# Spacers between the SBUF buffers of a two-layer encoder step: operands and one weight slot start 32 bytes into a 64-byte block

## The chip, the cores and the metric

The kernel runs on one NeuronCore of a Trainium2 chip, as one launch. The metric is the device time of the whole launch in microseconds. SBUF is the on-chip memory of 128 partitions; a buffer has the same start address in each partition, and all addresses below are bytes within a partition.

## The reference

One inference step of a two-layer encoder trunk for two request groups that share the weights: 256 prompt tokens and 32 sample tokens, model width 1024. Every layer adds four parts to the residual x:

```
x = x + 0.5 * swiglu(rmsnorm(x, norm_g[0]), w1g, w1u, w1d)      # width 2816
x = x + mix(rmsnorm(x, norm_g[1]))                              # layer 0: attention, layer 1: recurrent
x = x + 0.5 * swiglu(rmsnorm(x, norm_g[2]), w2g, w2u, w2d)
x = x + (p_i @ w_pe) * sigmoid(rmsnorm(x, norm_g[3]) @ w_pg)
```

The mixer of layer 0 is stick-breaking attention (16 heads of 64, with 256 past keys for the sample group). The mixer of layer 1 is a width-4 convolution, two block-diagonal gates (16 blocks of 80), a linear recurrence over time and a gelu gate, 1280 wide. A final rmsnorm follows. All inputs and outputs are float32.

## The kernel before, in words

**Layout.** Activations lie transposed: features on the 128 partitions, the 288 tokens (TOK) along the free axis, so a buffer such as `xg_hi` is 128 x 8 x 288. A weight matrix is cut into tiles of 128 x 128 that are the stationary operand of a matmul; a row block of 288 tokens is the moving operand. Both are 4 bytes per element.

**Three matmuls per tile.** Each float32 operand is split into a high part and a low part of the type float32r. `product` (L1086) multiplies one tile as hi x hi (L1090), moving low x weight high (L1091), moving high x weight low (L1092), all into one PSUM bank. Each of the three loads its stationary tile anew. What follows calls these three a tile.

**Phases.** `plan` (L72) lists the phases in order: up0, down0 (the first half-step), qkv, wo (attention), up1, down1, ple0, up2, down2, lru_in, gates, lru_g, lru_o, up3, down3, ple1. A phase is a row of groups; a group is one load of weights (16 tiles in up, qkv, lru_in; 11 in down; 10 in ple and lru_o; 13 in gates). Groups alternate between two slots, `raw0`, `w_hi0`, `w_lo0` and `raw1`, `w_hi1`, `w_lo1`. For a group ahead, SP loads the weights into `raw` (L303 on), ACT copies them rounded into `w_hi` (L476), and DVE subtracts to get `w_lo` (L736), each in two parts; TensorE waits for `w_lo_done`. ACT starts on a slot when TensorE is done with the group before in that slot (`tiles_done`), and SP loads when DVE is done with `raw`.

**Moving operands by phase.** Stages 0 to 3 and 5 to 7 read `xg_hi`, `xg_lo` (the residual times the norm's gain). Stage 4, that is up2, reads the second pair `xg_side_hi`, `xg_side_lo`. The down phases read `h_hi`, `h_lo`, wo reads `o_hi`, `o_lo`, gates reads `c_hi`, `c_lo` (292 columns instead of 288), lru_o reads `y_hi`, `y_lo`. A ple group has first two tiles on `p_hi`, `p_lo` and then eight on `xg_hi`, `xg_lo`.

**Where the buffers start.** `sb` (L147) takes buffers one behind the other; each begins at the next multiple of 32 bytes. The first, `x_res`, begins at 16512, a multiple of 64. A row of 288 tokens is 1152 bytes, 18 x 64, so each of a buffer's rows has the start of the buffer within a block of 64. Before the change `xg`, `raw`, `w_hi`, `w_lo`, `h`, `xg_side`, `o` and `y` all begin at a multiple of 64. `vecs_sb` holds 648 bytes, which puts `p_hi` and `p_lo` and all the small buffers behind them up to `mean_w` (`square`, `sum_squares`, `std`, `rstd`, `gate_in`, `gate_act`, `up_in`, `hidden0`, `hidden1`) in the middle, 32 bytes past a multiple of 64. A row of `c_hi` or `c_lo` is 1168 bytes, so its rows begin 0, 16, 32 and 48 bytes past one in turn. A weight tile is 512 bytes.

The scoped buffers (L185 to L223) share addresses: `h`, `xg_side`, `p_raw` and `first_squares` in one scope, the attention's in the next, the recurrent block's in a third.

Of the kernel before, what the change touches and what calls it, by code (L numbers as in the profile page):

```python
# [6 lines left out]
F32 = mybir.dt.float32  # L7
F32R = mybir.dt.float32r
# [3 lines left out]
P = 128  # L12
# [14 lines left out]
TOK = SEQ + DEC  # L27
KD = D_MODEL // P
# [115 lines left out]
def build(nc, a):  # L144
    ctx = ExitStack()
    with ctx:
        def sb(name, shape, dt=F32, scope=ctx):  # L147
            return scope.enter_context(nc.sbuf_tensor(name, shape, dt))
# [5 lines left out]


        x = sb("x_res", [P, KD, TOK])
        xg_main = (sb("xg_hi", [P, KD, TOK], F32R), sb("xg_lo", [P, KD, TOK], F32R))
        raw = [sb(f"raw{i}", [P, 2 * KD * P]) for i in range(2)]
        w_hi = [sb(f"w_hi{i}", [P, 2 * KD * P], F32R) for i in range(2)]
        w_lo = [sb(f"w_lo{i}", [P, 2 * KD * P], F32R) for i in range(2)]  # L160
        vecs = sb("vecs_sb", [P, sum(VECS.values())])
        vec, at = {}, 0
        for n, w in VECS.items():
# [19 lines left out]


        with ExitStack() as scope:  # L185
            h_hi = sb("h_hi", [P, KF, TOK], F32R, scope)
            h_lo = sb("h_lo", [P, KF, TOK], F32R, scope)
            xg_side = (sb("xg_side_hi", [P, KD, TOK], F32R, scope), sb("xg_side_lo", [P, KD, TOK], F32R, scope))
            p_raw = sb("p_raw", [P, 2 * KP, TOK], F32, scope)
            first_squares = sb("first_squares", [P, KD // 2, TOK], F32, scope)  # L190
        with ExitStack() as scope:
            o_hi = sb("o_hi", [P, KD, TOK], F32R, scope)
            o_lo = sb("o_lo", [P, KD, TOK], F32R, scope)
            q_all = sb("q_all", [P, PAIRS, TOK], F32, scope)
            k_all = sb("k_all", [P, PAIRS, KEYS], F32, scope)
            v_all = sb("v_all", [P, PAIRS, 3 * P], F32, scope)
            past_v = sb("past_v_sb", [P, PAST // P, D_MODEL], F32, scope)
            v_rows = [sb(f"v_rows{i}", [P, 3 * P], F32, scope) for i in range(2)]
            logit = [[sb(f"logit{i}{j}", [P, SCOLS], F32, scope) for j in range(2)] for i in range(2)]
            stay = [[sb(f"stay{i}{j}", [P, SCOLS], F32, scope) for j in range(2)] for i in range(2)]  # L200
            stay_hi = [[sb(f"stay_hi{i}{j}", [P, SCOLS], F32R, scope) for j in range(2)] for i in range(2)]
            stay_lo = [[sb(f"stay_lo{i}{j}", [P, SCOLS], F32R, scope) for j in range(2)] for i in range(2)]
            mask = sb("mask", [P, SCOLS], F32, scope)
            all_ones = sb("all_ones", [P, P], F32, scope)
            from_here = sb("from_here", [P, P], F32R, scope)
            ones = sb("ones", [P, P], F32R, scope)
            ident = sb("ident", [P, P], F32, scope)
# [1272 lines left out]
```

## Time and profile before

| | |
|---|---|
| median of 3 runs | 1229.05 us (1228.37 to 1229.31) |
| profiled execution | 1229.69 us |
| its span, first to last instruction | 1227.8 us |
| granted TensorE clock over the span | 0.990 of full |
| TensorE busy | 1188.5 us (97%) |
| VectorE (DVE) busy | 790.1 us (64%) |
| ScalarE (ACT) busy | 582.5 us (47%) |
| DMA | 193.20 MB, mean 157 GB/s |

The profiled execution lies 0.6 us above the median of the runs, and 1.9 us of it lie around the span. A matmul's bar in the profile overlaps the next one's, so the rate of TensorE is not read from the length of a bar but from the distance between the starts of two matmuls; this text calls that distance the pitch.

### The profile page before, as it was taken

Reading aid. Unit: us, or ns where it says so; the run is one execution under the profiler, and the core shown is the slowest. Engines: PE = TensorE matmul, PEld = TensorE weight load, DVE = VectorE, ACT = ScalarE, POOL = GpSimd, SP = SyncE. Lnnn points to the kernel's source line nnn. Section 1 sums busy time; section 2 is a strip of 40 time slices with the busy share of each in tenths; the row PEclk is TensorE's granted clock in tenths of the full one; section 3 lists DMA queues with packets and bytes.
Section 4 is the critical chain, followed back from the end, with each engine's and each line's share of the span. In section 5 each row is a group of like instructions: output and inputs, shape, how many; then the busy total and the mean of one; then the engine's idle time right before and its main releaser. Section 6 shows DMA issues by size and latency. Waiting matters only on the chain.

```text
span 1227.8 us, 23251 instructions
## 1 busy us (share of the span) xinstructions
PE 1188.5 (97%) x8952; PEld 1177.0 (96%) x8952; DVE 790.1 (64%) x1161; ACT 582.5 (47%) x860; POOL 177.4 (14%) x204
## 2 busy tenths in 40 slices
PE   6999999889999999999999999999996999999996
PEld 6999999889999999999999999999996999999996
DVE  7656555566649666655786666456889765665566
ACT  6444443445555444433564444344674544443353
POOL 3000011211124000002230000021245400000122
PEclk9999999899999999999999999999998999999998
DMA  6554444633343544444455444445452544444542
GB/s 221 181 171 156 145 152 165 240 104 104 104 146 138 176 166 171 150 145 162 153 191 183 155 165 149 160 148 195 147 172 88 188 171 165 152 152 143 181 145 96
DMA packets 35899, 193.20 MB, mean 157 GB/s; under 512 B 3808, under 2 KB 6128, under 8 KB 22784
## 3 DMA queue, kind: packets, MB, share of 16 engines
q1 hardware_dynamic: 34800, 187.86, 44.6%
q0 software_dynamic: 1040, 4.51, 1.1%
q8 instruction: 42, 0.69, 0.2%
q14 instruction: 17, 0.14, 0.0%
HBM read 188.78 MB, written 3.58 MB: 157 GB/s over the span
## 4 chain that ended last, share of the span: by engine, by line
PE 85%; DVE 7%; issue 2%; ACT 2%; POOL 2%; DMA 2%; SPq 0%; DVEq 0%; POOLq 0%; ACTq 0%
PE bank L1090 28%; PE bank L1092 27%; PE bank L1091 27%; DVE w_lo L736 2%; DMA raw<-in_up 1%; ACT w_hi L476 1%; PE bank L1135 1%; POOL sum_squares L341 1%; DVE xg_lo L745 1%; PE bank L1121 1%; DVE u_ext L868 1%; POOL gated L427 1%; DMA raw<-in_lru_o 0%; DVE y_lo L859 0%; DVE u_ext L870 0%
## 5 line engine op out<-in xcount | busy, mean ns | idle before, releaser
L476 ACT ACTIVATE w_hi<-raw 128x1024 fp32r<-128x1024 f32 (+2 forms) x410 | 370.4, 927 | 364.4 <-PE bank L1092 345.2
L736 DVE TENSOR_TENSOR w_lo<-raw,w_hi 128x1024 fp32r<-128x1024 f32 (+2 forms) x410 | 452.8, 1122 | 91.5 <-ACT w_hi L476 88.5
L1090 PE MATMUL bank<-xg_hi,w_hi 128*128 128x288 f32 x1536 | 460.1, 300 | 14.4 <-DVE w_lo L767 8.7
L1091 PE MATMUL bank<-xg_lo,w_hi 128*128 128x288 f32 x1536 | 455.6, 297 | 0.0
L1092 PE MATMUL bank<-xg_hi,w_lo 128*128 128x288 f32 x1536 | 454.1, 296 | 0.0
L1090 PEld LDWEIGHTS bank<-xg_hi,w_hi 128*128 128x128 f32 x1536 | 290.2, 189 | 17.1 <-issue 8.7
L1092 PEld LDWEIGHTS bank<-xg_hi,w_lo 128*128 128x128 f32 x1536 | 291.7, 190 | 0.0
L1091 PEld LDWEIGHTS bank<-xg_lo,w_hi 128*128 128x128 f32 x1536 | 290.9, 189 | 0.3
L1090 PE MATMUL bank<-h_hi,w_hi 128*128 128x288 f32 x704 | 208.4, 296 | 0.0
L1091 PE MATMUL bank<-h_lo,w_hi 128*128 128x288 f32 x704 | 207.7, 295 | 0.0
L1092 PE MATMUL bank<-h_hi,w_lo 128*128 128x288 f32 x704 | 207.0, 294 | 0.0
L909 DVE TENSOR_TENSOR gate_in<-bank,rstd 128x288 f32<-128x288 f32 x88 | 40.3, 458 | 177.9 <-PE bank L1092 177.6
L1092 PEld LDWEIGHTS bank<-h_hi,w_lo 128*128 128x128 f32 x704 | 132.6, 188 | 0.0
L1091 PEld LDWEIGHTS bank<-h_lo,w_hi 128*128 128x128 f32 x704 | 132.2, 188 | 0.0
L1090 PEld LDWEIGHTS bank<-h_hi,w_hi 128*128 128x128 f32 x704 | 131.9, 187 | 0.0
L1090 PE MATMUL bank<-xg_side_hi,w_hi 128*128 128x288 f32 x352 | 104.5, 297 | 0.0
L1091 PE MATMUL bank<-xg_side_lo,w_hi 128*128 128x288 f32 x352 | 103.8, 295 | 0.0
L1092 PE MATMUL bank<-xg_side_hi,w_lo 128*128 128x288 f32 x352 | 103.5, 294 | 0.0
L351 POOL TENSOR_TENSOR sum_squares<-x_res 128x288 f32<-128x288 f32 x8 | 6.2, 779 | 614.3 <-DVE x_res L759 614.3
L481 ACT ACTIVATE xg_hi<-x_res,vecs_sb 128x288 fp32r<-128x288 f32 (+1 forms) x56 | 28.9, 532 | 125.8 <-DVE x_res L759 123.2
L344 POOL TENSOR_TENSOR square<-x_res 128x288 f32 (+1 forms) x58 | 44.5, 767 | 242.5 <-DVE x_res L759 241.0
L1092 PEld LDWEIGHTS bank<-xg_side_hi,w_lo 128*128 128x128 f32 x352 | 66.3, 188 | 0.0
(186 smaller groups left out, 1275.9 us busy)
## 6 DMA issues: line engine op xcount, KB each, us to landing
raw<-in_up SPq DMA_DIRECT2D x87, 1024.0 KB, 4.8
raw<-in_down SPq DMA_DIRECT2D x64, 704.0 KB, 4.0
raw<-in_qkv SPq DMA_DIRECT2D x24, 512.0 KB, 4.4
raw<-in_ple SPq DMA_DIRECT2D x16, 640.0 KB, 3.8
raw<-in_lru_in SPq DMA_DIRECT2D x6, 1024.0 KB, 4.9
raw<-in_lru_o SPq DMA_DIRECT2D x8, 640.0 KB, 3.8
raw<-in_wo SPq DMA_DIRECT2D x4, 1024.0 KB, 4.9
raw<-in_lru_g SPq DMA_DIRECT2D x4, 1024.0 KB, 4.9
```

The lines of the kernel that those rows point to most:

```text
L341: nc.gpsimd.tensor_tensor(sum_squares[:], sum_squares[:], term, ALU.add).then_inc(summed_squares, 1)
L344: nc.gpsimd.tensor_tensor(square[:], x[:, k, :], x[:, k, :], ALU.mult).then_inc(squared, 1)
L427: nc.gpsimd.tensor_tensor((a_square, gated)[half][:, m, :], rate[:, half * HALF + m, :], rate[:, half * HALF + m, :], ALU.mult).then_inc(a ...
L476: nc.scalar.activation(w_hi[slot][:, cols], raw[slot][:, cols], ACT.Copy).then_inc(w_hi_done, 1)
L481: nc.scalar.activation(xg_of(stage)[0][:, k, :], x[:, k, :], ACT.Copy, scale=gain[:, stage, one(k)]) \
L736: nc.vector.tensor_tensor(w_lo[slot][:, cols], raw[slot][:, cols], w_hi[slot][:, cols].bitcast(F32), ALU.subtract).then_inc(w_lo_done, 1)
L745: nc.vector.scalar_tensor_tensor(out=dst, in0=src, scalar=scalar, in1=hi.bitcast(F32), op0=ALU.mult, op1=ALU.subtract).then_inc(done, 1)
L868: nc.vector.tensor_tensor_scan(u_ext[:, m, 0:SEQ], rate[:, m, 0:SEQ], conv[:, m, 0:SEQ], 0.0, ALU.mult, ALU.add)
L909: nc.vector.tensor_tensor(gate_in[:], first, rstd[:], ALU.mult).then_inc(gate_in_done, 1)
L1090: nc.tensor.matmul(out, w_hi[slot][:, cols], hi[:, k, 0:width], start=start, stop=False)
L1091: nc.tensor.matmul(out, w_hi[slot][:, cols], lo[:, k, 0:width], start=False, stop=False)
L1092: return nc.tensor.matmul(out, w_lo[slot][:, cols], hi[:, k, 0:width], start=False, stop=stop)
```

## The change

Spacer buffers that nothing reads or writes are allocated between the others, and the two weight slots are taken in the order hi0, lo0, hi1, lo1 instead of hi0, hi1, lo0, lo1. No instruction, wait, loop or transfer is added or taken away. The recurrent block's scope has no spacer.

```diff
         x = sb("x_res", [P, KD, TOK])
+        sb("gap0", [P, 8])
         xg_main = (sb("xg_hi", [P, KD, TOK], F32R), sb("xg_lo", [P, KD, TOK], F32R))
+        sb("gap1", [P, 8])
         raw = [sb(f"raw{i}", [P, 2 * KD * P]) for i in range(2)]
-        w_hi = [sb(f"w_hi{i}", [P, 2 * KD * P], F32R) for i in range(2)]
-        w_lo = [sb(f"w_lo{i}", [P, 2 * KD * P], F32R) for i in range(2)]
+        w_hi, w_lo = [sb("w_hi0", [P, 2 * KD * P], F32R)], [sb("w_lo0", [P, 2 * KD * P], F32R)]
+        sb("gap2", [P, 8])
+        w_hi.append(sb("w_hi1", [P, 2 * KD * P], F32R))
+        w_lo.append(sb("w_lo1", [P, 2 * KD * P], F32R))
+        sb("gap3", [P, 8])
         vecs = sb("vecs_sb", [P, sum(VECS.values())])
...
         with ExitStack() as scope:
+            sb("gap_h", [P, 4], F32, scope)
             h_hi = sb("h_hi", [P, KF, TOK], F32R, scope)
             h_lo = sb("h_lo", [P, KF, TOK], F32R, scope)
-            xg_side = (sb("xg_side_hi", [P, KD, TOK], F32R, scope), sb("xg_side_lo", [P, KD, TOK], F32R, scope))
+            sb("gap_side", [P, 12], F32, scope)
+            xg_side = [sb("xg_side_hi", [P, KD, TOK], F32R, scope)]
+            sb("gap_side_lo", [P, 8], F32, scope)
+            xg_side.append(sb("xg_side_lo", [P, KD, TOK], F32R, scope))
...
         with ExitStack() as scope:
+            sb("gap_o", [P, 8], F32, scope)
             o_hi = sb("o_hi", [P, KD, TOK], F32R, scope)
+            sb("gap_o_lo", [P, 8], F32, scope)
             o_lo = sb("o_lo", [P, KD, TOK], F32R, scope)
```

With the rule of 32 bytes the starts within a block of 64 bytes become:

| buffer | before | after |
|---|---|---|
| x_res, raw0, raw1 | 0 | 0 |
| xg_hi, xg_lo | 0, 0 | 32, 32 |
| w_hi0, w_lo0 | 0, 0 | 0, 0 |
| w_hi1, w_lo1 | 0, 0 | 32, 32 |
| p_hi, p_lo and the small buffers | 32 | 32 |
| h_hi, h_lo | 0, 0 | 32, 32 |
| xg_side_hi, xg_side_lo | 0, 0 | 32, 0 |
| o_hi, o_lo | 0, 0 | 32, 0 |
| y_hi, y_lo | 0, 0 | 0, 0 |
| c_hi, c_lo (first row) | 0, 32 | 0, 32 |
| q_all, k_all, v_all, logit and the rest of the attention | 0 | 0 |

## Rows read from the trace of the kernel before

**Rows 1.** The page: busy time by engine, slices of the span, shares of the chain.

```profile
PE 1188.5 (97%) x8952; PEld 1177.0 (96%) x8952; DVE 790.1 (64%) x1161; ACT 582.5 (47%) x860; POOL 177.4 (14%) x204
...
PEclk9999999899999999999999999999998999999998
...
PE 85%; DVE 7%; issue 2%; ACT 2%; POOL 2%; DMA 2%; SPq 0%; DVEq 0%; POOLq 0%; ACTq 0%
```

**Rows 2.** Groups on TensorE: line, out<-in, shapes, count | busy us, mean ns | idle before.

```profile
L1090 PE MATMUL bank<-xg_hi,w_hi 128*128 128x288 f32 x1536 | 460.1, 300 | 14.4 <-DVE w_lo L767 8.7 <-DVE q_all L779 3.1 <-DVE xg_lo L745 1.9
...
L1090 PE MATMUL bank<-h_hi,w_hi 128*128 128x288 f32 x704 | 208.4, 296 | 0.0
...
L1090 PE MATMUL bank<-xg_side_hi,w_hi 128*128 128x288 f32 x352 | 104.5, 297 | 0.0
...
L1090 PE MATMUL bank<-y_hi,w_hi 128*128 128x288 f32 x80 | 25.2, 315 | 9.3 <-DVE y_lo L859 6.2 <-DVE w_lo L736 3.1
...
L1090 PE MATMUL bank<-o_hi,w_hi 128*128 128x288 f32 x64 | 19.4, 303 | 0.4 <-DVE x_res L759 0.4
```

**Rows 3.** Waits: engine, line, whom it waited for: us in total, times, longest.

```profile
ACT w_hi L476 <- PE bank L1092: 345.2, 134, 8.6
...
DVE gate_in L909 <- PE bank L1092: 177.6, 79, 3.0
...
ACT w_hi L476 <- DMA raw<-in_up: 7.1, 5, 2.9
```

**Rows 4.** Timeline of TensorE in up0: start us, bar us, engine, line, operation.

```profile
40.06 0.29 PE L1090 MATMUL bank<-xg_hi,w_hi 128*128 128x288 f32 x1
...
52.86 0.29 PE L1090 MATMUL bank<-xg_hi,w_hi 128*128 128x288 f32 x1
```

**Rows 5.** Timeline of TensorE in the ple0 phase, start to start.

```profile
605.03 0.29 PE L1090 MATMUL bank<-p_hi,w_hi 128*128 128x288 f32 x1
...
618.58 0.29 PE L1090 MATMUL bank<-xg_hi,w_hi 128*128 128x288 f32 x1
618.70 0.29 PE L1091 MATMUL bank<-xg_lo,w_hi 128*128 128x288 f32 x1
...
624.96 0.29 PE L1090 MATMUL bank<-p_hi,w_hi 128*128 128x288 f32 x1
```

**Rows 6.** Timeline of TensorE in the gates phase: its first and second matmul, and the first behind it.

```profile
879.58 0.30 PE L1090 MATMUL bank<-c_hi,w_hi 128*128 128x292 f32 x1
879.72 0.30 PE L1091 MATMUL bank<-c_lo,w_hi 128*128 128x292 f32 x1
...
900.43 0.29 PE L1090 MATMUL bank<-xg_hi,w_hi 128*128 128x288 f32 x1
```

**Rows 7.** Timeline of TensorE as its clock rises after the up0 phase.

```profile
239.77 0.44 PE L1090 MATMUL bank<-xg_hi,w_hi 128*128 128x288 f32 x1
240.01 0.44 PE L1091 MATMUL bank<-xg_lo,w_hi 128*128 128x288 f32 x1
```

**Rows 8.** Groups on DVE that write a row of 288 columns.

```profile
L910 DVE TENSOR_TENSOR up_in<-bank,rstd 128x288 f32<-128x288 f32 x88 | 39.4, 448 | 0.0
...
L995 DVE TENSOR_TENSOR gate_g<-bank,rstd 128x288 f32<-128x288 f32 x10 | 4.1, 442 | 1.3 <-PE bank L1092 1.3
```

**Rows 9.** Busy us by engine (and count) in two stretches, clock, DMA share, GB/s.

```profile
240.00:400.00 160.00, 154.27 (x1283) 148.00 (x1283) 104.22 (x165) 87.12 (x137) 34.98 (x33) 0.99 0.35 119
...
860.00:970.00 110.00, 100.70 (x734) 99.34 (x733) 93.90 (x145) 68.11 (x103) 47.48 (x49) 0.97 0.41 141
```

**Rows 10.** DMA issues: transfer, count, KB each, median us from issue to landing.

```profile
raw<-in_up SPq DMA_DIRECT2D x87, 1024.0 KB, 4.8
```

## The prediction

> **What bounds the kernel now.** I read the page first: TensorE is busy 97% of the span and carries 85% of the chain that ended last; DVE carries 7%, ACT, POOL and DMA 2% each [rows 1]. The waits agree: ACT waits 345.2 us in total for TensorE to give a weight slot back, and DVE 177.6 us for the sums of an up group, while ACT waits for a load in the up phases for only 7.1 us [rows 3]. A 1 MB load of an up group lands in 4.8 us [rows 10], and the group's 48 matmuls take 6.4 us (below), so transfers are early. TensorE's own rate sets the time, and the rest stands behind it.
>
> So the next view is that rate. The groups of TensorE give the counts: 1536 tiles on xg, 704 on h, 352 on xg_side, 80 on y, 64 on o, three matmuls each [rows 2]; gates has 52 and ple 32 by the code. The bars (about 300 ns) overlap and say nothing of the rate. The timeline does: from 40.06 to 52.86 us lie 96 matmuls, 12.80 us, a pitch of 133.3 ns [rows 4]. At the full clock of 2.4 GHz 288 columns are 120.0 ns, so each matmul takes 13.3 ns, or 32 cycles, more than its columns. This is no fixed cost of an instruction: while the clock was granted at its lower level (1.2 GHz), the pitch is 0.24 us, just its 288 columns [rows 7]. The pitch is also strikingly even: of the triples of matmuls that follow each other without a wait, more than nine in ten take 400 ns to the nanosecond. Something besides the columns holds TensorE back at full clock, and reading operands from SBUF is a candidate. That is what an address can change.
>
> **What the change does, part by part.** No instruction goes or comes. The counts, waits and bytes stay.
>
> *Moving operands.* The trace of before has one operand that already starts mid-block: p. Five ple groups, from 605.03 to 624.96 us, are 150 matmuls in 19.93 us [rows 5]. At the pitch of [rows 4] they would take 20.00 us. They hold 10 tiles on p and 40 on xg, with the same code, slots and clock; the missing 0.067 us are 6.7 ns per p tile, or 2.2 ns per matmul (131.1 ns instead of 133.3). Some of it falls in the xg tiles just behind, where the pitch swings (0.12 us once in [rows 5]) before it is even again, as it also does behind a stall. So p is a disturbance of six matmuls, and what a long stretch of displaced rows settles to is not shown. The second sample is the gates phase, whose rows start at 0, 16, 32 and 48: 156 matmuls of 292 columns in 20.85 us, 133.7 ns [rows 6]. Four more columns are 1.7 ns, so against 133.3 + 1.7 = 135.0 it gains 1.3 ns per matmul; if the columns are not what counts, it loses 0.3 ns.
>
> The bounds for a displaced matmul: below, 120 ns, its columns; above, 140 ns, which the first two of gates show (0.14 us, [rows 6]) and which is also what a count of 16-column blocks gives. (320 cycles are 20 such blocks, 18 of them the row; a displaced row touches 19, so 21 blocks, 336 cycles, 140 ns. The p rows speak against it.) I take the p rows' 2.2 ns, the nearest: same length, same displacement, same instruction.
>
> What it applies to: xg and h, 2240 tiles, all three matmuls displaced: 2240 x 6.7 ns = 15.0 us. xg_side and o, 416 tiles, where the high part is displaced and the low part not, so two matmuls of three: 416 x 2/3 x 6.7 = 1.9 us. y, c and p stay where they are: 0. Together 16.9 us.
>
> *The weight slot.* Slot 1 holds half of the groups, and there weight and moving operand both start mid-block (but for xg_side_lo and o_lo). No row of before shows this: all weight slots start at 0. Two readings are open: what counts is the moving operand's own start (then both slots gain), or that the two reads start apart (then slot 0 alone gains, since in slot 1 both are shifted alike and stand to each other as before). I take the first, by a little, since p's tiles gain in slot 0 and slot 1 alike, and keep the second as a rival.
>
> *What absorbs it.* In the attention (240 to 400 us) TensorE is busy 154.3 of 160 us, in the recurrent block 100.7 of 110 [rows 9]; the chain there runs through DVE and ACT at times. The first holds 192 tiles of qkv and 64 of wo: 256 x 6.7 ns = 1.7 us, of which I strike half, 0.9 us. Elsewhere TensorE has no one to wait for: with a pitch of 131.1 an up group takes 6.29 us, and the 1 MB load lands in 4.8 us.
>
> *DVE, ACT, POOL, SP.* The writes to xg, h, o, w_hi1 and w_lo1 move to mid-block. DVE writes a row mid-block in 448 ns (up_in) and at a block's start in 442 ns (gate_g), both from a bank and rstd [rows 8]: 6 ns, and 1% even of DVE's 7% of the chain is 0.9 us at most; DVE idles 177.6 us for TensorE in the up phases [rows 3], which hides it. I cost it at 0, with 0.9 us kept as the end if that cover goes. The raw buffers move by 64 bytes and stay at a block's start: 0 for the loads, which have 1.6 us of slack per up group. Slots interleaved as hi0, lo0, hi1, lo1 change no instruction: 0.
>
> **The sum.** -16.9 + 0.9 = -16.0 us on the profiled 1229.69 us, that is 1213.7; the median of the runs lies 0.6 us lower, so 1213.
>
> A rule of the Trainium skill speaks against any effect. "SBUF — State Buffer", Specifications, says that SBUF is read in lines of 16 bytes and that crossing into new lines is what costs; 32 bytes are two whole lines, so a displaced row crosses as many as before. By that the sum is 0 and the time 1229; the p rows, 6.7 ns per tile, disagree. "TensorE: Matmul & The Clock Gate", Step-by-step, also has the moving operand and the weight load on two independent read ports, with nothing to collide. Its Back-to-back issue gap puts 288 columns at 122.5 ns; this trace has 133.3, so something that the rule lacks is at work.
>
> **The rivals.**
> *Slot 0 alone gains* (the two reads must start apart): half of the sum, -8 us, 1221. For: it explains why the even 400 ns comes with equal starts, and why the gates, where the starts differ by turns, are in between. Against: nothing in the rows of before.
> *Nothing* (the p rows' gain is a passing disturbance, and long stretches settle at 400 ns again): 1229. For: xg's pitch behind a stall swings as well and then settles. This is what both rules above would give. A change that doesn't do what it says is part of this: if the starts that matter were in units other than 64 bytes, p would not have differed.
> *A new, lower level.* Behind a stall or behind p single pitches are 0.12 us [rows 5], so TensorE can start matmuls closer. If displaced rows settle near 126 ns, 7 ns go from each of 2240 x 3 + 416 x 2 = 7552 matmuls: -53 us, 1176.
> *Slower: slot 1 pays.* In slot 1 weight tile and row both straddle blocks: 9 blocks instead of 8 and 19 instead of 18. If those matmuls, half of 7552, take the 140 ns of [rows 6], that is 3776 x 6.7 = +25 us, less 8 us that slot 0 gains: +17, 1246. It decides from the point where slot 1's pitch passes 135.5 ns, as much above 133.3 as slot 0's is below. For: no row shows both displaced; the gates' worst pitches. Against: p pays nothing for straddling.
>
> **How the numbers follow.** The forecast (1213) has a chance of 0.30, slot 0 alone 0.20, nothing 0.22, the lower level 0.11, slower 0.17. About 0.2%, or 2.5 us, is what a measurement of this kernel can tell from no change. Faster by more than that: 0.30 + 0.20 + 0.11 = 0.61; within it 0.22; slower 0.17. The forecast's own range is 1206 to 1219 (1.3 to 3.2 ns per matmul). The range of 8 in 10 leaves out the lower level's centre and the worse half of the slower case: 1196 to 1240.
>
> **What would show it.** In the timeline of up0 and down0 the pitch over 96 matmuls: 131 ns in both slots for the forecast; 131 in one and 133.3 in the other for the rival of the slots; 133.3 throughout for nothing; above 135 in slot 1 for the slower case. xg_side and o should gain two thirds of it, y nothing, and the 400 ns of y should stand unchanged in the same trace. DVE and ACT groups should keep their mean durations within 1 to 2%, and DVE's and ACT's waits for TensorE should shrink by about the gain. The forecast is wrong if the even 400 ns comes back with displaced rows, or if the time moves while the pitch does not.

## The result, and the profile after

The changed kernel takes 1220.92 us (median of 3 runs, 1220.75 to 1221.01) against 1229.05 us: a ratio of 0.9937, with a 95% interval of 0.9923 to 0.995. Beside a later kernel, on one chip, the changed one came to 1220.29 us, ratio 0.9928 (0.9914 to 0.9941). So it is faster by 8 us, half of the 16 us that were forecast.

The page of the changed kernel, the same lines as [rows 1] without the clock's:

```profile
span 1219.3 us, 23251 instructions
...
PE 1181.0 (97%) x8952; PEld 1170.2 (96%) x8952; DVE 790.8 (65%) x1161; ACT 583.3 (48%) x860; POOL 177.5 (15%) x204
...
PE 88%; DVE 5%; issue 2%; ACT 2%; POOL 1%; DMA 1%; SPq 0%; DVEq 0%; POOLq 0%; ACTq 0%
```

TensorE is busy 7.5 us less; DVE and ACT are busy as before to within 0.8 us, so the writes into displaced buffers cost nothing that shows. The waits answer to [rows 3]:

```profile
ACT w_hi L488 <- PE bank L1104: 343.5, 135, 7.4
...
DVE gate_in L921 <- PE bank L1104: 173.5, 79, 3.0
```

DVE's wait for TensorE in the up phases shrinks by 4.1 us and ACT's by 1.7 us, less than the 8 us of the gain. The pitch is read as in [rows 4]. The timeline of TensorE (start us, bar us) in two neighbouring groups of up0, slot 0 and then slot 1, each of 48 matmuls; then up2, from its third group to its end (320 tiles); then up3 in the same way, and down3 (176 tiles):

```profile
39.04 0.30 PE L1102 MATMUL bank<-xg_hi,w_hi 128*128 128x288 f32 x1
...
45.39 0.30 PE L1102 MATMUL bank<-xg_hi,w_hi 128*128 128x288 f32 x1
...
51.74 0.30 PE L1102 MATMUL bank<-xg_hi,w_hi 128*128 128x288 f32 x1
...
637.30 0.30 PE L1102 MATMUL bank<-xg_side_hi,w_hi 128*128 128x288 f32 x1
...
764.50 0.30 PE L1102 MATMUL bank<-h_hi,w_hi 128*128 128x288 f32 x1
...
977.98 0.30 PE L1102 MATMUL bank<-xg_hi,w_hi 128*128 128x288 f32 x1
...
1104.91 0.30 PE L1102 MATMUL bank<-h_hi,w_hi 128*128 128x288 f32 x1
...
1174.68 0.29 PE L1102 MATMUL bank<-p_hi,w_hi 128*128 128x288 f32 x1
```

Both slots take 6.35 us per group, against 6.40: slot 0 and slot 1 gain alike. A tile in up3 takes (1104.91 - 977.98) / 320 = 396.7 ns, in down3 396.4, in up2, whose low rows begin elsewhere than its high rows, 397.5. The same stretch of up3 before the change:

```profile
984.71 0.30 PE L1090 MATMUL bank<-xg_hi,w_hi 128*128 128x288 f32 x1
...
1112.71 0.30 PE L1090 MATMUL bank<-h_hi,w_hi 128*128 128x288 f32 x1
```

128.00 us, 400.0 ns a tile. At 3.3 ns less, 2820 tiles give 9.4 us at most; the span is 8.5 us shorter. Not every phase gains 3.3 ns: over all phases, the tiles that follow each other without a wait take 399.88 ns in the mean before and 396.93 ns after, and 2820 times the difference is 8.3 of the 8.5 us. So practically all of the gain is TensorE's pitch; waits have at most a few tenths of a microsecond in it.

### The profile page after: what moved, and what is told of

Its sections match the earlier page's. It is cut to its first block, busy times and chain, and to the rows that moved or that the text cites. A ratio compares the mean times of both kernels' runs of the same rounds, so it can differ in the third digit from the quotient of the medians.

```text
span 1219.3 us, 23251 instructions
## 1 busy us (share of the span) xinstructions
PE 1181.0 (97%) x8952; PEld 1170.2 (96%) x8952; DVE 790.8 (65%) x1161; ACT 583.3 (48%) x860; POOL 177.5 (15%) x204
## 4 chain that ended last, share of the span: by engine, by line
PE 88%; DVE 5%; issue 2%; ACT 2%; POOL 1%; DMA 1%; SPq 0%; DVEq 0%; POOLq 0%; ACTq 0%
PE bank L1102 29%; PE bank L1104 28%; PE bank L1103 28%; DVE w_lo L748 2%; ACT w_hi L488 1%; PE bank L1147 1%; PE bank L1133 1%; DVE u_ext L880 1%; DMA x_res<-in_x 1%; POOL gated L439 1%; DVE xg_lo L757 1%; DVE u_ext L882 0%; POOL a_square L439 0%; DMA raw<-in_up 0%; PE bank L1174 0%
## 5 line engine op out<-in xcount | busy, mean ns | idle before, releaser
L1102 PEld LDWEIGHTS bank<-xg_side_hi,w_hi 128*128 128x128 f32 x352 | 66.2, 188 | 0.2
```

Of the source, the lines that this page charges most:

```text
L1102: nc.tensor.matmul(out, w_hi[slot][:, cols], hi[:, k, 0:width], start=start, stop=False)
```

## The experiments

Four theories came up in turn. Theory 1: a moving row that starts in mid-block is read faster (what the forecast assumed). Theory 2: row and weight tile must start apart within a block of 64. Theory 3: the displaced slot 1 makes the gain. Theory 4, formed after the first four experiments: what counts is the distance from the row's start to the weight tile's start modulo 128. This text calls it d, the weight's start less the row's. Before the change d is 0 everywhere but for the rows of p and of gates. After it d is 32 in slot 0 and 64 in slot 1, for xg and h; for the diff's spacers move the weights too, by more than the rows. In up2 after the change the high rows have d = 96 in slot 0 and 0 in slot 1, the low rows 64 and 96. The p rows of the kernel before have d = 96.

**e1_rows_only.** The spacers around the rows alone; the diff is against the changed kernel, the later ones against the kernel before.

```diff
-        sb("gap2", [P, 8])
-        sb("gap3", [P, 8])
-            sb("gap_side", [P, 12], F32, scope)
+            sb("gap_side", [P, 16], F32, scope)
```

> The rows move as in the change (xg, h at 32; the high parts of xg_side and o at 32), both weight slots stay at 0. Theory 1, the row's own start decides: a tile takes 396.6 ns in both slots as after the change, time 1220 to 1222. Theory 2, row and weight tile must start apart: here they are apart in both slots, so both gain more than after the change, 393 to 394 ns (the 6.7 ns of the p rows), 1213 us. Theory 3, the shift of slot 1 makes the gain: 400 ns in both slots, 1229.

Measured: 1225.95 us, ratio 0.9977 (0.9967 to 0.9987), single runs from 1223 to 1229. First matmul of the third group of up3, first of down3, first behind down3:

```profile
979.17 0.30 PE L1101 MATMUL bank<-xg_hi,w_hi 128*128 128x288 f32 x1
...
1106.11 0.30 PE L1101 MATMUL bank<-h_hi,w_hi 128*128 128x288 f32 x1
...
1176.51 0.30 PE L1101 MATMUL bank<-p_hi,w_hi 128*128 128x288 f32 x1
```

xg gains as after the change (396.7 ns, both slots), but h, in mid-block too, does not: 400.0 ns here in down3, and 403 ns in down1 and down2 of the same trace, slower than before. Theory 1 can't give that. By address h stands at d = 96 in this kernel, xg at d = 32. The trace is of the fastest of the nine runs (1223.24 us), so it does not show why others took up to 6 us longer.

**e2_slot1_only.** No spacer but these two.

```diff
+        sb("gap_1", [P, 8])
         w_hi.append(sb("w_hi1", [P, 2 * KD * P], F32R))
         w_lo.append(sb("w_lo1", [P, 2 * KD * P], F32R))
+        sb("gap_2", [P, 8])
```

> Only w_hi1 and w_lo1 move to 32, all rows stay at 0. Theory 1 (the row's own start): 400 ns, 1229 us. Theory 2 (apart): slot 1 gains, slot 0 stays at 400 ns, a mean of 397 to 398 ns, 1221 to 1224 us. Theory 3 (slot 1's shift): 396.6 ns in both slots, 1221 us.

Measured: 1224.99 us, ratio 0.9969 (0.9958 to 0.9981). In up0, slot 0's group and slot 1's:

```profile
38.73 0.29 PE L1096 MATMUL bank<-xg_hi,w_hi 128*128 128x288 f32 x1
...
45.12 0.29 PE L1096 MATMUL bank<-xg_hi,w_hi 128*128 128x288 f32 x1
...
51.47 0.30 PE L1096 MATMUL bank<-xg_hi,w_hi 128*128 128x288 f32 x1
```

6.39 us in slot 0 (d = 0), 6.35 in slot 1 (d = 32), though neither xg nor h is in mid-block. Theories 1 and 3 fall; this is what theory 2 said of the up phases. In the down phases theory 2 fails too. There h begins at a block's start, as slot 0's weights do, and only slot 1's weights are in mid-block. Down3, slot 0's group and slot 1's, of 11 tiles each:

```profile
1117.46 0.29 PE L1096 MATMUL bank<-h_hi,w_hi 128*128 128x288 f32 x1
...
1121.82 0.30 PE L1096 MATMUL bank<-h_hi,w_hi 128*128 128x288 f32 x1
...
1126.23 0.29 PE L1096 MATMUL bank<-h_hi,w_hi 128*128 128x288 f32 x1
```

It is slot 0 that gains (4.36 us; the mean over the phase is 396.9 ns a tile), and slot 1 that does not (4.41 us, 400.7 ns; before it is 4.40 us). By address h has d = 64 in slot 0 and 96 in slot 1.

**e3_all_mid.** Rows as in the change, both weight slots displaced alike.

```diff
+        sb("gap_3", [P, 8])      # ahead of w_hi0, and one more behind w_lo1; the rest as in e1_rows_only
```

> Rows as in the change and both weight slots at 32: rows and weights start alike, but in mid-block. Theory 1 (the row's own start): 396.6 ns in both slots, 1221 us. Theory 2 (apart): xg and h stand to the weights as before the change, 400 ns, only the low parts of xg_side and o are apart, 1227 to 1229 us. Theory 3 (slots that differ from each other): 400 ns, 1229.

Measured: 1222.68 us, ratio 0.9946 (0.9929 to 0.9962). Up2 (side rows), then up3:

```profile
639.44 0.30 PE L1103 MATMUL bank<-xg_side_hi,w_hi 128*128 128x288 f32 x1
...
767.44 0.30 PE L1103 MATMUL bank<-h_hi,w_hi 128*128 128x288 f32 x1
...
981.00 0.29 PE L1103 MATMUL bank<-xg_hi,w_hi 128*128 128x288 f32 x1
...
1107.93 0.29 PE L1103 MATMUL bank<-h_hi,w_hi 128*128 128x288 f32 x1
```

xg and weights both start in mid-block and gain all the same (396.7 ns): theory 2 falls as well. Here d is 64, because the spacer ahead of the raw buffers adds 32. Up2 doesn't gain (400.0 ns); its high rows have d = 0. Nor does lru_o (400 ns), whose rows have d = 96.

**m1_table.** The three matmuls per tile alone, on constant data, no other engine at work, with every pair of starts.

```diff
+CASES = [(a, a, b, TOK, TOK) for a in (0, 16, 32, 48) for b in (0, 16, 32, 48)]
+hi = hi_rows[:, at_hi // 4 + k * step:at_hi // 4 + k * step + n]
+nc.tensor.matmul(to, w_hi[:, cols], hi, start=k == 0, stop=False)
```

> A table of the pitch alone: TensorE runs the kernel's three matmuls per tile on constant data, nothing else runs, and the rows and weight tiles begin 0, 16, 32 or 48 bytes (and some 64, 96, 128) past a multiple of 256, 96 matmuls for each pair; then 256 to 320 columns at two starts. All of the model is left out; the outputs are zeros. Theory 1: the pitch depends on the row's start alone: 133.3 ns at 0, 132.2 or 131 at 32, whatever the weights' start. Theory 2: it depends on the difference: 133.3 where both are the same, less where not. Either way (0, 0) should give 133.3 ns if nothing but these two reads is at work, and 122.5 or less if the other engines and the transfers cause the excess. Over the columns: a fixed excess gives columns / 2.4 GHz + 13.3 ns; a grid of 16 or 64 cycles gives steps.

In the columns' part of the table the rows lie 1280 bytes apart instead of 1152. The last 72 matmuls of (rows 0, weights 0), of (32, 0), of 256 columns and of 288 columns with rows 1280 bytes apart:

```profile
17.94 0.30 PE L63 MATMUL bank<-hi_rows,w_lo 128*128 128x288 f32 x1
...
27.54 0.29 PE L63 MATMUL bank<-hi_rows,w_lo 128*128 128x288 f32 x1
...
119.64 0.30 PE L63 MATMUL bank<-hi_rows,w_lo 128*128 128x288 f32 x1
...
129.32 0.29 PE L63 MATMUL bank<-hi_rows,w_lo 128*128 128x288 f32 x1
...
399.74 0.28 PE L63 MATMUL bank<-hi_rows,w_lo 128*128 128x256 f32 x1
...
408.38 0.28 PE L63 MATMUL bank<-hi_rows,w_lo 128*128 128x256 f32 x1
...
460.13 0.29 PE L63 MATMUL bank<-hi_rows,w_lo 128*128 128x288 f32 x1
...
469.61 0.29 PE L63 MATMUL bank<-hi_rows,w_lo 128*128 128x288 f32 x1
```

9.60 / 72 = 133.3 ns: the excess over 120 ns is there with TensorE alone, so neither the other engines nor the transfers cause it. It is not a fixed excess, though. At (0, 0) it is 13.3 ns at 256 and at 320 columns too (120.0 and 146.7 ns), but 10.0 ns at 264 and 15.0 ns at 284. And 288 columns give 131.7 ns, not 133.3, once the rows lie 1280 bytes apart. That is one sample, but it says that the distance between rows may count as well, which theory 4 leaves out. In the kernels the rows lie 1152 bytes apart, but for those of gates.

(32, 0), the p rows' pair, settles at 9.68 / 72 = 134.4 ns, slower than (0, 0). Among multiples of 32 the table goes by d: 133.3 ns at d = 0 for the pairs (0, 0), (32, 32), (64, 64), (128, 0); 132.2 at d = 64 for (0, 64), (64, 0), (32, 96), (96, 32); 132.2 at d = 32 for (0, 32), (32, 64), (96, 0). Steps of 16 don't keep to it: (16, 16) has 132.2. The lowest is 131.1, at (0, 48) and (32, 16).

Theory 4 comes from this table, and it orders the phases of the three kernels above: 396.7 ns at d = 32 and 64, 400 at 0, 400 to 403 at 96. It has no account of phases whose high and low rows have different distances. One is up2 after the change; a group of slot 1 and then one of slot 0:

```profile
669.08 0.29 PE L1102 MATMUL bank<-xg_side_hi,w_hi 128*128 128x288 f32 x1
...
675.46 0.30 PE L1102 MATMUL bank<-xg_side_hi,w_hi 128*128 128x288 f32 x1
...
681.80 0.29 PE L1102 MATMUL bank<-xg_side_hi,w_hi 128*128 128x288 f32 x1
```

Slot 0, with d = 96 for its high rows and 64 for its low ones, takes 6.34 us (396.2 ns a tile over the phase), slot 1, with 0 and 96, takes 6.38 us (398.8 ns). The same pair, 0 and 96, ran at 400.0 ns in e3_all_mid.

**e4_weights_64_on and e5_one_gap_32** set theories 1 and 4 against each other from both sides.

```diff
+        sb("gap_1", [P, 16])    # e4: ahead of w_hi0, and one more behind w_lo1
```

> No row and no weight tile in mid-block: two spacers of 64 bytes put both weight slots 64 bytes past a multiple of 128, while xg, h, xg_side, o and y stay at a multiple of 128. Theory 1 (mid-block starts make the gain): nothing moved to mid-block, 400 ns per tile, 1229 us. Theory 4 (what counts is the distance of row start and weight tile start modulo 128): the distance is 64 everywhere, as in slot 1 after the change, 396.7 ns in all phases, also up2 and lru_o, which the change left above it; 2820 tiles x 3.3 ns = 9.4 us, 1219 to 1220 us.

```diff
+        sb("gap_1", [P, 8])     # e5: ahead of xg_hi, the only spacer
```

> One spacer of 32 bytes behind x_res, so that every row and every weight tile behind it begins in mid-block and keeps its distance to the others. Theory 1 (mid-block starts make the gain): 396.7 ns, 1221 us. Theory 4 (the distance modulo 128): the distance stays 0, 400 ns, 1228 to 1230 us.

Measured: e4, with nothing moved to mid-block, 1220.14 us, ratio 0.9927 (0.991 to 0.9943), as fast as the change. e5, with all of it in mid-block, 1229.4 us, ratio 1.0004 (0.9994 to 1.0013), no change. Up2 and up3 of e4:

```profile
636.96 0.29 PE L1096 MATMUL bank<-xg_side_hi,w_hi 128*128 128x288 f32 x1
...
763.89 0.29 PE L1096 MATMUL bank<-h_hi,w_hi 128*128 128x288 f32 x1
...
977.48 0.29 PE L1096 MATMUL bank<-xg_hi,w_hi 128*128 128x288 f32 x1
...
1104.41 0.29 PE L1096 MATMUL bank<-h_hi,w_hi 128*128 128x288 f32 x1
```

and up3 of e5:

```profile
983.71 0.30 PE L1095 MATMUL bank<-xg_hi,w_hi 128*128 128x288 f32 x1
...
1111.70 0.30 PE L1095 MATMUL bank<-h_hi,w_hi 128*128 128x288 f32 x1
```

396.7 ns in both of e4's, 400.0 in e5. Both came out as theory 4 said. The middle of a block of 64 has no part in the gain, and since e5 takes the weight buffers in the new order too, that order has none either.

**m2_fine and m3_mixed.** The bare stream again, with finer, wider and mixed pairs.

```diff
+CASES += [(0, 0, w, w, TOK, TOK, P) for w in range(8, 128, 8)]         # m2
+CASES += [(0, 0, 0, 0, TOK, TOK, w) for w in (96, 64, 32)]             # m2: narrower weight tiles
+CASES = [(0, 0, v, w, TOK, TOK, P) for v in W for w in W]              # m3, W = (0, 8, 16, 48, 64, 112)
```

> The table again, 144 matmuls for each pair, weights in steps of 8 bytes against rows at 0, in steps of 16 against rows at 8 and 16, and narrower weight tiles (96, 64, 32 columns) at (0, 0). The model is left out; the outputs are zeros. Theory 4: a shift of both by 32 changes nothing, distance 0 gives 133.3, 64 and 96 (weights 64 or 32 ahead of the rows) give 132.2, rows 32 ahead of the weights 134.4 ns once a stretch is long, while its first six matmuls may look like the p rows of the kernel before. The first 16-byte table had 131.1 ns with weights 48 ahead; finer steps show whether less is to be had. If the 13.3 ns over the columns are the weight load's share of the reads, they shrink with the tile's columns: 10, 6.7 and 3.3 ns for 96, 64 and 32.

> The bare stream again, 144 matmuls for each pair: weight highs and lows at different starts, low rows at other starts than high rows, and seven more weight starts. The model is left out; the outputs are zeros. If each matmul's pitch goes by its own distance alone, a mixed pair lies between the two even pairs (131.1 and 133.3 give 131.8 or 132.6), and nothing is below 131.1. If the order of three matters, some pair falls outside.

The weight tile's width has a small part in the excess. With 96, 64 and 32 columns instead of 128 the pitch at (0, 0) is 132.2, 131.7 and 131.1 ns. At 32 columns that is an excess of 11 ns, where one proportional to the width would be 3.3. From 711.06 to 723.64 us lie 96 of these matmuls:

```profile
711.06 0.29 PE L66 MATMUL bank<-hi_rows,w_lo 128*32 128x288 f32 x1
...
723.64 0.29 PE L66 MATMUL bank<-hi_rows,w_lo 128*32 128x288 f32 x1
```

With rows 1152 bytes apart (0, 0) came to 133.3 and (0, 64) to 132.2 each time. But one pair can settle in more than one rhythm, that is, in another repeating pattern of pitches: (0, 48) ran at 131.1 twice and at 133.3 in m3, (0, 8) at 131.1 and then at 134.4, (32, 0) at 134.4 and then at 133.3. What ran ahead of it differed. (0, 112) came to 131.1 both times. No mixed pair fell below 131.1. But mixed pairs do not lie between the two even ones, as they would if each matmul's pitch went by its own distance alone: with the rows at 0, weight highs at 16 and lows at 48 ran at 131.1 ns, where 16 and 48 throughout ran at 132.2 and 133.3 in the same trace; highs at 16 and lows at 112 ran at 133.3, where 16 and 112 throughout gave 132.2 and 131.1.

**e6_weights_48_on, e7_weights_72_on, after_again.** Rows at a multiple of 128, the weight tiles at one distance, through a view into a longer buffer.

```diff
+        sb("gap_1", [P, 8])      # e7: 16
+        w_buf = [sb(n, [P, 2 * KD * P + 32], F32R)[:, 4:4 + 2 * KD * P] for n in ("w_hi0", "w_lo0", "w_hi1", "w_lo1")]   # e7: from 2
+        sb("gap_2", [P, 24])     # e7: 16
```

> Rows of xg, h, xg_side, o and y at a multiple of 128, all weight tiles 48 bytes past one, the distance at which the bare stream ran at 131.1 ns twice. Theory 4 (the distance sets the pitch) with the bare stream as its measure: 393.3 ns per tile, 6.7 ns below before on 2820 tiles, -18.8 us, 1210 us. If the bare stream is no guide because ACT, DVE and the transfers read and write beside it: 396 to 400 ns, 1219 to 1229 us.

> The changed kernel beside e6_weights_48_on on one chip: 1221 us, 0.993 to 0.994 of before, by every theory; it is the measure that a better layout has to beat.

> The same with the weight tiles 72 bytes past a multiple of 128, where the bare stream ran at 134.45 ns: by theory 4 403.3 ns per tile, +9.4 us, 1238 us, slower than before by as much as the change was faster. By theory 1 (a start at a multiple of 64 is what costs) no tile starts at one, so faster than before.

Measured: e6 1223.92 us, ratio 0.996 (0.9946 to 0.9973), 398.0 ns a tile; e7 1215.91 us, ratio 0.9892 (0.9877 to 0.9908), faster than the change where theory 4 expected slower. after_again came to the 1220.29 us given above. Up3 of e7:

```profile
974.61 0.29 PE L1093 MATMUL bank<-xg_hi,w_hi 128*128 128x288 f32 x1
...
1101.01 0.30 PE L1093 MATMUL bank<-h_hi,w_hi 128*128 128x288 f32 x1
```

126.40 / 320 = 395.0 ns. Both expectations from the bare stream missed (393.3 and 403.3 ns). e7 is faster, as the form of theory 1 in its expectation said (a start at a multiple of 64 is what costs), but e4, with all starts at one, had refuted that already. d modulo 128 alone is thus not the whole rule.

**e8_72_packed, e9_112_packed, e10_rows_32_ahead.**

```diff
+        w_all = sb("w_all", [P, 4 * 2 * KD * P + 32], F32R)     # e8: from element 2, gaps 16 and 16
+        w_buf = [w_all[:, 4 + n * 2 * KD * P:4 + (n + 1) * 2 * KD * P] for n in range(4)]   # e9: gaps 24 and 8
```

> As e7_weights_72_on, but the four weight buffers lie 8192 bytes apart, so that highs and lows start alike modulo 256, as in the bare stream; in e7 they lay 8320 apart, 128 off each other modulo 256. If that is why e7 ran at 395 ns where the bare stream gave 403.3: 403.3 ns here, 1238 us. If the bare stream does not carry over to this distance at all: 395 ns, 1216 us.

> Weights 112 bytes past a multiple of 128, 8192 bytes apart; the bare stream settled at 131.1 ns there both times. If a distance with one stable rhythm in the bare stream carries over: 393.3 ns per tile, 1210 us. If it does not: anything between 395 and 402 ns, 1216 to 1233 us.

```diff
+        sb("gap_1", [P, 24])     # e10: ahead of w_hi0, and one of 8 behind w_lo1
```

> Every row starts 32 bytes ahead of its weight tiles modulo 128 (rows at 0, weights at 96), the distance of the p rows of the kernel before, now for whole phases. If the p rows' rate holds for long stretches, as the prediction took it: 393.3 ns per tile, 1210 us. If their gain was a passing one: the 400 to 403.3 ns that the bare stream and the down phases of e1_rows_only settled to at this distance, 1229 to 1238 us.

Measured: e8 1221.07 us, ratio 0.9945 (0.9924 to 0.9967), 396.7 ns: neither of the two values expected. Its four runs lie at 1219.1, 1219.2, 1222.9 and 1223.5 us, all above e7's four (1215.6 to 1216.9); the trace is of the fastest. The step between the buffers does count (395.0 in e7), but it doesn't bring the bare stream's 403.3. e9 1212.75 us, ratio 0.9873 (0.9856 to 0.9889), the fastest, with the pitch that the bare stream gave; its ple phases (395.4 ns) and gates gain less, so the time stays above the 1210 us expected. e10 1235.05 us, ratio 1.0051 (1.0034 to 1.0067), slower than before. Up3 of e9:

```profile
971.33 0.29 PE L1094 MATMUL bank<-xg_hi,w_all 128*128 128x288 f32 x1
...
1097.20 0.29 PE L1094 MATMUL bank<-h_hi,w_all 128*128 128x288 f32 x1
```

and of e10, with down3 behind it:

```profile
988.50 0.29 PE L1096 MATMUL bank<-xg_hi,w_hi 128*128 128x288 f32 x1
...
1117.56 0.30 PE L1096 MATMUL bank<-h_hi,w_hi 128*128 128x288 f32 x1
...
1187.96 0.29 PE L1096 MATMUL bank<-p_hi,w_hi 128*128 128x288 f32 x1
```

393.3 ns in e9. In e10 403.3 ns in up3 and 400.0 in down3, one distance with two rhythms in one trace, as in the bare stream. The operand is not what decides between them, for up0 of the same trace, on xg as up3 is, runs at 400.0 ns.

All layouts beside each other, with the up3 stretch of each trace (one execution) and the median of all its runs:

| kernel | d of xg, slot 0 / slot 1 | ns per tile, up3 | median us | ratio |
|---|---|---|---|---|
| before | 0 / 0 | 400.0 | 1229.05 | 1 |
| e5_one_gap_32 | 0 / 0 | 400.0 | 1229.4 | 1.0004 |
| the change | 32 / 64 | 396.7 | 1220.92 | 0.9937 |
| e1_rows_only | 32 / 32 (h: 96) | 396.7 | 1225.95 | 0.9977 |
| e2_slot1_only | 0 / 32 (h: 64 / 96) | 398.1 | 1224.99 | 0.9969 |
| e3_all_mid | 64 / 64 | 396.7 | 1222.68 | 0.9946 |
| e4_weights_64_on | 64 / 64 | 396.7 | 1220.14 | 0.9927 |
| e6_weights_48_on | 48 / 48 | 398.0 | 1223.92 | 0.996 |
| e7_weights_72_on | 72 / 72 | 395.0 | 1215.91 | 0.9892 |
| e8_72_packed | 72 / 72 | 396.7 | 1221.07 | 0.9945 |
| e9_112_packed | 112 / 112 | 393.3 | 1212.75 | 0.9873 |
| e10_rows_32_ahead | 96 / 96 | 403.3 | 1235.05 | 1.0051 |

## Where the prediction was right, and the step that failed

**Right.** That TensorE's pitch sets the time and that it can be moved by addresses alone: 8.3 of the 8.5 us are pitch. That the other engines, the loads and the new order of the slots cost nothing: e5_one_gap_32 has the new order and the time of before, and DVE's groups keep their means (up_in 448 and gate_g 442 ns, as in [rows 8]). Nor did the attention and the recurrent block swallow much: 2820 tiles at 3.3 ns would be 9.4 us, and the span gave 8.5. That both slots gain came true as well, but not for the reason given.

**The step that failed** is "I take the p rows' 2.2 ns, the nearest: same length, same displacement, same instruction". Measured was 1.1 ns per matmul (396.7 instead of 400.0 ns per tile). The p rows were the same in what was thought to matter, and different in what did: their d was 96, and xg's became 32 and 64. The p rate was also a passing one, held for six matmuls. Held for whole phases, d = 96 gives 400 to 403.3 ns and a slower kernel (e10_rows_32_ahead).

The size failed because the mechanism under it did. The prediction took it that "what counts is the moving operand's own start"; e5_one_gap_32 puts xg and h in mid-block and gains nothing, and e4_weights_64_on keeps both at the start of a block and gains all of it. The table of the change, which counts starts within 64 bytes, hid the point: by it row and weight tile of slot 1 "stand to each other as before", but within 128 bytes they moved 64 apart. The prediction saw a danger in the rate ("what a long stretch of displaced rows settles to is not shown") and priced it only as the rival *nothing*. By its own terms 15.0 + 1.9 us at 3.3 ns instead of 6.7 are 8.4 us, which is close to the result: the counts were right, the rate was not. That it comes out so near is in part luck. Up2 gained 2.5 ns a tile and not by its displaced high rows alone, and y, put at 0 with 400 ns "unchanged", moved as well, because its weights did: lru_o runs at 397.1 ns in slot 0 (d = 64) and 399.2 in slot 1 (d = 96).

**The rivals.** *Slot 0 alone gains* named 1221, the measured time, by luck: each slot gains half as much, rather than half of the slots all of it. Its idea that the two reads must stand apart was nearer to the truth than the forecast's, with the wrong unit. *Nothing* is wrong in its time; and its last sentence, that units other than 64 bytes would have left p unmoved, was the trap, for p moved and the unit is not 64. *A new, lower level* was not found: no layout with 288 columns settled below 131.1 ns. *Slot 1 pays* is refuted: its tiles straddle blocks and gain.

**The Trainium skill.** "SBUF — State Buffer", Specifications, with its lines of 16 bytes, and "TensorE: Matmul & The Clock Gate", Step-by-step, with two independent read ports, give no reason why layouts that are displaced by whole lines should differ. e9_112_packed (393.3 ns) and e10_rows_32_ahead (403.3 ns), 112 and 96 bytes on, do differ: the pitch depends on how the starts of row and weight tile stand to each other. What in the hardware makes it so, no run here shows.

## What to carry to other kernels

In a stream of matmuls with a fresh weight load each, look at the pitch per tile to the nanosecond, over whole phases; if it stands a few per cent above columns / clock, try the distance between the weight buffers and the moving buffers, not the alignment of either. Spacers and the start of a view moved this kernel from 0.987 to 1.005 of its time, with nothing but addresses changed. Don't take a rate from a handful of matmuls: p's six ran fast at a distance that is slow in the long run; and measure the layout in the kernel itself, for of four distances taken from the bare stream (48, 72, 112, 96) two did not carry over.

## What the runs showed of the hardware that was not expected

- With TensorE alone at work, a fresh weight tile for each matmul and full clock, the pitch exceeds the columns by 13.3 ns at d = 0 with rows 1152 bytes apart, and, both starts at 0, by 10.0 to 15.0 ns for 256 to 320 columns with rows 1280 bytes apart; weight tiles of 32 columns still have 11 ns (m1_table, m2_fine).
- Settled pitches are mostly one of 131.1, 131.7, 132.2, 133.3 and 134.4 ns, with rhythms that repeat after one tile (400.0 ns in [rows 4]) or a few. One layout can fall into different rhythms (403.3 and 400.0 ns in e10_rows_32_ahead); that what ran before decides which is not shown, only that it differed. That this is also why single runs of e1_rows_only (1223 to 1229 us), e2_slot1_only (1222.5 to 1228.8) and e8_72_packed differ is likely but not shown.
- What makes the pitch depend on the starts, and why weight buffers 8320 bytes apart (e7_weights_72_on, 395.0 ns) and 8192 apart (e8_72_packed, 396.7 ns) differ, stays open. Both this step and the one between rows (1152 or 1280 bytes) change where reads start modulo 256; no run here separates a rule modulo 256 from one modulo 128.
